# Second block: ScalarE makes the probabilities' high part before the exponentials, the weight split moves to the step's end, and the keys' chunk gets its own PSUM bank

## The reference

```
h = rms_norm(x);  proj = h @ w_in               # 6 MoBA heads, 6 dilated heads: q, k, v, gate; 4 memory heads: q, gate
q, k = rope(rms_norm(q)), rope(rms_norm(k))      # per head of 64; no rope in the memory branch
o = softmax(q k^T * scale + mask) v              # masked causal / dilated; memory: 256 keys from another input
y = o * silu(gate)                               # all heads side by side
x = x + y @ w_out
```

## Time and profile before

| | |
|---|---|
| median of 3 runs | 2871.37 us (2870.94 to 2874.71) |
| the profiled execution | 2871.01 us, of which 2869.1 us from the first to the last instruction (the span) |
| PE busy | 2545.6 us, 89% of the span |
| PE weight loads (beside the matmuls) | 2033.6 us |
| DVE busy | 1314.1 us |
| POOL busy | 1129.0 us |
| ACT busy | 1074.0 us |
| mean granted clock of TensorE | 0.943 of full speed |

### The profile page before, as it was taken

One profiled execution on the slowest core, in us unless ns is written; L12 is line 12 of the kernel. 1 busy time (PEld: TensorE's weight loads), 2 busy tenths in 40 slices (PEclk: granted clock), 3 DMA queues, 4 the chain that ended last, 5 costly groups with the idle time before them and its releaser, 6 DMA issues.

```text
span 2869.1 us, 31223 instructions
## 1 busy us (share of the span) xinstructions
PE 2545.6 (89%) x11290; PEld 2033.6 (71%) x11290; DVE 1314.1 (46%) x2101; ACT 1074.0 (37%) x1530; POOL 1129.0 (39%) x828
## 2 busy tenths in 40 slices
PE   6999999589999999999996899999877668878677
PEld 5887887367887888878774788878656556656556
DVE  5544034735542054430547344513675553664652
ACT  4333143534332143321435343323553532553431
POOL 3545445124544445544460245544421312421312
PEclk9999999789999999999996999999988888989889
DMA  4222222102222222222230122223211111221111
GB/s 151 88 102 88 103 102 105 42 33 98 89 102 88 97 94 90 100 96 95 102 118 15 44 103 92 98 94 126 81 66 42 54 52 44 81 66 44 52 52 59
DMA packets 37470, 233.25 MB, mean 81 GB/s; under 512 B 5632, under 2 KB 5632, under 8 KB 10624
## 3 DMA queue, kind: packets, MB, share of 16 engines
q1 hardware_dynamic: 30816, 218.12, 21.1%
q10 hardware_dynamic: 6560, 13.84, 1.7%
HBM read 223.55 MB, written 2.10 MB: 79 GB/s over the span
## 4 chain that ended last, share of the span: by engine, by line
issue 63%; POOL 37%; POOLq 1%
POOL w_lo L412 37%; POOLq L406 0%; POOLq L410 0%; POOLq L202 0%; POOLq L412 0%; POOLq L1771 0%
## 5 line engine op out<-in xcount | busy, mean ns | idle before, releaser
L412 POOL TENSOR_TENSOR w_lo<-raw,w_hi 128x512 fp32r<-128x512 f32 x824 | 1128.8, 1401 | 1739.6 <-ACT w_hi L852 1739.3
L420 PE MATMUL ps<-h_hi,w_hi 128*128 128x512 f32 x2304 | 934.1, 405 | 51.1 <-DVE h_lo L1223 20.7
L421 PE MATMUL ps<-h_lo,w_hi 128*128 128x512 f32 x2304 | 911.8, 396 | 0.0
L422 PE MATMUL ps<-h_hi,w_lo 128*128 128x512 f32 x2304 | 910.5, 395 | 0.0
L852 ACT ACTIVATE w_hi<-raw 128x1024 fp32r<-128x1024 f32 x412 | 413.5, 1052 | 879.0 <-PE ps L422 835.2
L420 PEld LDWEIGHTS ps<-h_hi,w_hi 128*128 128x128 f32 x2304 | 442.7, 192 | 159.4 <-DVE h_lo L1223 23.8
L421 PEld LDWEIGHTS ps<-h_lo,w_hi 128*128 128x128 f32 x2304 | 442.4, 192 | 94.2 <-issue 5.3
L422 PEld LDWEIGHTS ps<-h_hi,w_lo 128*128 128x128 f32 x2304 | 441.0, 191 | 95.3
L420 PE MATMUL ps<-hid_hi,w_hi 128*128 128x512 f32 x704 | 277.0, 393 | 7.5 <-DVE hid_lo L1223 7.5
L422 PE MATMUL ps<-hid_hi,w_lo 128*128 128x512 f32 x704 | 281.5, 400 | 0.0
L421 PE MATMUL ps<-hid_lo,w_hi 128*128 128x512 f32 x704 | 278.1, 395 | 0.0
(11 more groups left out here) (264 smaller groups left out, 2548.6 us busy)
## 6 DMA issues: line engine op xcount, KB each, us to landing
raw<-in_stream SPq DMA_DIRECT2D x206, 1024.0 KB, 4.8
hraw<-xs ACTq DMA_DIRECT2D x96, 64.0 KB, 2.1
x_sb<-in_x ACTq DMA_DIRECT2D x1, 2048.0 KB, 10.3
out_x<-x_sb SPq DMA_DIRECT2D x8, 256.0 KB, 2.7
mem_sb<-in_mem ACTq DMA_DIRECT2D x1, 1024.0 KB, 13.0
rec_sb<-in_recip ACTq DMA_DIRECT2D x2, 512.0 KB, 4.5
memn<-in_mem ACTq DMA_DIRECT2D x1, 1024.0 KB, 4.9
dist_sb<-in_dist ACTq DMA_DIRECT2D x2, 448.0 KB, 3.3
```

What stands on the lines that cost most here:

```text
L412: ins = gp.tensor_tensor(w_lo[:, s, c], raw[:, s, c], w_hi[:, s, c].bitcast(F32), ALU.subtract)
L420: pe.matmul(dst, l_hi, r_hi, start=first, stop=False)
L421: pe.matmul(dst, l_hi, r_lo, start=False, stop=False)
L422: return pe.matmul(dst, l_lo, r_hi, start=False, stop=last)
```

## The change

Four edits, all in the second block. On PE the k chunk (c = 1) goes to bank 6 instead of bank 4; the wait for the squares moves from ahead of the matmuls of step 2 to ahead of `mean(0)`, and for step 4 the wait ahead of the matmuls is for the q chunk's squares only, that for the k chunk's ahead of `mean(1)`. On ACT `turn(j)` reads bank 4 + 2j; in each step pt_hi comes ahead of the exponentials; and the split in step 4 comes behind both.

```diff
-                    if s in (2, 4):
-                        pe.wait_ge(hn_in, 2 * G + s // 2)
+                    if s == 4:
+                        pe.wait_ge(hn_in, 2 * G + 1)
...
-                        mm = three(ps[:, 4 if c < 3 else 7, :], w[0][:, k, c % 2, :], w[1][:, k, c % 2, :],
+                        mm = three(ps[:, (4, 6, 4, 7)[c], :], w[0][:, k, c % 2, :], w[1][:, k, c % 2, :],
...
                     if s == 2:
+                        pe.wait_ge(hn_in, 2 * G + 1)
                         pe.wait_ge(gate_raw, 7 * l + gi - 1)
                         mean(0)
                     if s == 4:
+                        pe.wait_ge(hn_in, 2 * G + 2)
                         pe.wait_ge(hn_ms, 2 * G + 1)
                         mean(1)
...
@@ ScalarE, attention_step: ahead of the exponentials
+                unit = lagged(here, before, s, LAG_TR)
+                if unit:
+                    stage, u = unit
+                    b, kbs = u % TB, stage.widths[u] // P
+                    act.wait_ge(t_tr, stage.u0 + u + 1)
+                    if b == 0 and (u or not stage.memory):
+                        act.wait_ge(t_o, stage.outs0 + u // TB)
+                    if stage.memory:
+                        src = ps[:, 2 + u % 2, :].rearrange("p (h k n) -> p h k n", h=2, k=2)
+                    else:
+                        src = ps[:, 2:4, 0:P * kbs].rearrange("p h (k n) -> p h k n", k=kbs)
+                    act.activation(pt_hi[:, :, 0:kbs, P * b:P * b + P], src, ACT.Copy).then_inc(t_thi, 1)
                 unit = lagged(here, before, s, 0)
...
                     ins.then_inc(t_exp, 1)
...
@@ the same lines are taken out here, and instead:
+                if produce and s == 4:
+                    produce(s, True)
...
@@ ScalarE, producer
-                    act.activation(xs[:, j, :], ps[:, 4, :], ACT.Copy, scale=g).then_inc(xs_ready, 1)
-                    act.activation(sq[:, j, :], ps[:, 4, :], ACT.Square).then_inc(hn_in, 1)
+                    act.activation(xs[:, j, :], ps[:, 4 + 2 * j, :], ACT.Copy, scale=g).then_inc(xs_ready, 1)
+                    act.activation(sq[:, j, :], ps[:, 4 + 2 * j, :], ACT.Square).then_inc(hn_in, 1)
...
-                def step(s):
+                def step(s, spare=False):
...
-                    if s == 4:
+                    if s == 4 and spare:
+                        split(p + 2, 0)
+                    elif s == 4:
                         act.wait_ge(panel_done, p + 1)
                         turn(1)
-                        split(p + 2, 0)
```

## The result

The changed kernel takes 2810.52 us, the median of four runs (2807.05 to 2811.19), against 2872.45 for the kernel before beside it (2870.94 to 2874.71): ratio 0.9781 [0.9764, 0.9798]. The forecast was 2820 in 2800 to 2848. The profiled execution took 2807.05 us, its span 2805.2; against the 2871.01 of before that is 64.0 us where the sum said 50.6. The changed kernel's is the lowest of its four runs; the medians lie 61.9 us apart.

What follows compares the result with a forecast made beforehand. It took the group's period to be bound by a chain, PE to the end of step 3, then ACT and DVE. Terms 30 + 7.6 + 13 = 50.6 us off 2871.0 gave 2820.4, forecast as 2820, range 2800 to 2848.

Steps and rivals of the forecast that it cites:

- ordinary groups: Ten attention groups, gi 2 to 6 in two layers: 3.0 us less in each, 30 us together.
- rival A: Step 5: the rotation misses w_lo, so DVE waits once or never; 2800 us, with one wait 2810; chance 0.15.
- memory stages: gi 1 in two layers: PE's 3.79 us step-5 stop for exponentials goes; 3.8 us each, 7.6 for two.
- last stages: gi 7 in two layers: PE's and DVE's waits for pt_hi shrink; 6.5 us each, 13 for two.
- start of the block: Start of the second block: no change forecast, 0 us.
- pt_hi in front, step 6: Ordinary group: pt_hi directly behind newt removes DVE's 2.34 us wait; the closing run starts 2.5 us earlier.
- The rotation meets w_lo: Step 5, ordinary group: two rotation operations on DVE each wait 0.98 us beside POOL's w_lo, 2.0 us lost.
- B: Rival: DVE stands through all of w_lo, taking 7.3 us; a group keeps 0.6 us, total 2844; chance 0.15.
- late split: Steps 4 and 5: ms starts 2.2 us earlier, but the rotation beside w_lo costs 2.0.
- Up to the end of step 3: Ordinary group: PE's stops of 0.34 (bank) and 0.44 us (pt_hi) go, 0.8 us, and all that follows moves along.
- Rival C: PE's granted clock falls in the ordinary groups as idle time moves; at 0.76 there, 2906 us; chance 0.04.

Runs made afterwards that it cites:

- `pthi_only`: The kernel before with only the activation that writes pt_hi put ahead of the exponentials; 2814.64 us, ratio 0.9796 to the kernel before.
- `parts8`: The changed kernel with w_lo made in eight instructions of 256 columns instead of four of 512; 2783.34 us, ratio 0.9687 to the kernel before.
- `split_only`: The kernel before with only the split of step 4 moved behind the exponentials and pt_hi; 2870.19 us, ratio 0.999 to the kernel before.
- `no_bank`: The changed kernel with the key chunk back in bank 4 and the squares' waits in their old places; 2815.34 us, ratio 0.9796 to the kernel before.
- `bank_only`: The kernel before with only bank 6 for the keys and the moved waits; 2872.53 us, ratio 1.0002 to the kernel before.
- `last_warm`: The kernel before plus unread matmuls at steps 0, 3, 5 and 7 of the two last stages; 2863.72 us, ratio 0.997 to the kernel before.
- `warm`: The changed kernel with step 7's split moved behind the next step 0's exponentials, plus 26 unread matmuls ending each ordinary group; 2756.1 us, 0.9603 to the kernel before.

## Why the prediction was right, and where it was off

The measured time lies in the stated range, 9.5 us below the forecast, and the mechanism is the one forecast for the ordinary groups. The total alone would not have shown that: rival A with one wait gives 2810, which is what was measured. The rows rule it out (two waits). Of the 13.4 us by which the sum fell short, 2.8 are in the ordinary groups, 3.05 in the memory stages and 8.8 in the last stages, less 1.3 at the start of the block.

**pt_hi in front, step 6.** Right, and by `pthi_only` nearly the whole gain. The 2.34 us wait is gone, pt_hi follows ACT's newt directly, the exponentials' table load hides behind DVE's work, and what is late next is DVE.

**The rotation meets w_lo.** Right in place, number and size: two operations with 1.62 and 1.78 us, so 0.94 and 1.10 longer than 0.68, where 0.98 each was taken. Rivals A and B fell by these rows: there are two waits and not one or none, and w_lo took 5.49 us and not 7.3. "SBUF — State Buffer" in the Trainium skill, section "SBUF: two separate sides", says that whichever of the two engines starts first holds the shared ports for its whole instruction, and the other fully blocks. The runs agree in kind: with pieces of half the size (`parts8`) the wait shrinks. The measured prices stay below a whole w_lo instruction (5.15 / 4 = 1.29 us).

**What the late split is worth.** The text counted 2.2 us for ms and 2.0 against it in the rotation, so that DVE was free "practically where it was". The runs agree: `split_only` 0.999, `no_bank` no better than `pthi_only`, and in the rows ms 2.15 us earlier and the rotation 2.05 longer. So the 2.34 us of pt_hi carry the gain of a group's second half, and the split's move carries none of it.

**Up to the end of step 3: 0.34 + 0.44.** The size was about right, the reason was not. The text let all that follows hang on PE reaching the end of step 3. In the kernel before the chain ran through the first rotation, which holds the buffer that turn(1) refills. The bank's 0.34 was thus worth nothing alone (`bank_only`), and 4.8 us (a difference just outside the runs' spread), or 0.4 per stage, once pt_hi had moved that rotation. The ordinary groups gave 32.8 for the 30 forecast; gi 2 gave 0.8 us in the first layer and -0.2 in the second, the others 2.6 to 5.5, so 3.0 was right only as a mean. In gi 2 the new stop of 2.32 us takes most of the gain back; the prediction took all ten groups for one form, and did not look at where the split of step 7 falls in the memory stage. What spreads the others was not tried; up to 1.7 us of it is seen between two traces of the same stage.

**Memory stages, 7.6 against 10.65.** The 3.79 us stop of the earlier trace rows went, to 0.24. Its size was taken as the whole, with 4.6 as the upper end; both stages gave more (5.05 and 5.60). But PE's stops up to qk_lo were 0.61, 0.34, 3.79 and 3.08 before, 7.82 in all, and are 4.86 after, so 3.0 of the first stage's 5.05 us are stops (3.7 of 5.60 in the second). The other 2.1 lie near the 1.9 by which its matmuls are shorter (39.22 less 37.28). That the clock does this is argued from the rows; no run tried it in this stage, and the same stage is 1.0 us shorter in the trace of `last_warm`, which leaves it as it was.

**Last stages, 13 against 21.8.** The upper end was 14 for the pair. The waits came as forecast: 12.67 - 6.60 = 6.1 us of stops against 6.5, and 7.0 in the second layer. What the step left out is that the short stops also held the clock down: 0.77 before, 0.89 after. `last_warm` got 3.1 and 4.6 us out of the clock alone, and with these the stops make 9.2 and 11.6, beside the measured 11.5 and 10.3. The 8.8 us that this pair gave above its term are most of the 13.4 by which the sum fell short. Rival C had the right quantity with the wrong sign: it priced a clock that falls in the ordinary groups. There it stayed where it was, and in the other stages it rose, because stops of 1 to 4 us went.

**What stays open.** How much of what `warm` fell short of is the first rotation's hold on the DMA issue; no run moved that rotation alone. What makes the first block of `parts8` 7.5 us shorter and its last stages longer. And the clock's share in the memory stages.

## What to carry to other kernels

Where an in-order engine serves two readers, put first the operation whose reader stands directly ahead of the chain that closes the period; moving a load that another engine cannot share only moves who waits for it. An edit's worth depends on what binds after the others: the same bank was worth 0 and then some 4.8 us, so price edits in the order in which they free the chain. Look at each stage form by itself, and at the seams between them: an earlier split met att only behind the memory stage. Where PE has several stops of 1 to 4 us, the clock adds to what removing them gives: here 6 to 7 us of stops brought some 3 to 5 more. Where the long stop stayed and only stops under 1 us went, as in the ordinary groups, it added nothing.

## What the runs showed of the hardware

- A DVE operation that reads and writes SBUF alone waits for up to one POOL instruction of 512 columns (1.29 us), whether it has 256 or 512 columns itself: 1.62 and 1.78 us instead of 0.68 in the rotation, 1.45 and 1.35 instead of 0.35 for the two att of 256 columns, 1.60 and 1.75 for the closing products and 1.06 and 1.21 with POOL's pieces halved. An operation that reads PSUM and one SBUF tensor did not wait: ms takes 0.68 us at 2264.17, with w_lo running from 2262.06 to 2267.55. The closing run is 9.9 us with w_lo beside it, 7.6 in halves, and 5.9 without. I had not expected that the smaller pieces would pay for their greater number.
- The granted clock rose where stops of 1 to 4 us got fewer and shorter, with the long stop ahead of them nearly as long as before: in a last stage from 0.77 to 0.89, and in a memory stage from 0.91 to 0.95. Matmuls that nobody reads, put into such stops, raised a last stage from 0.76 to 0.85, and put into the stop at a group's end raised ordinary groups from 0.89 to 0.98. In ordinary groups that lost only stops of 0.34 to 0.90 us it stayed (0.874 and 0.879). Nor does it set their time: over the ten groups it is 0.90 in `pthi_only` and 0.86 in `no_bank`, and the kernels take 2814.64 and 2815.34 us.
